# Attention scores of a pair's second head placed earlier in a hand-ordered stream, and the turning of a row placed behind the next row's maximum

## The reference, cut to what matters

```python
proj = h @ w_in
qA, qB = _split_q(proj[..., :Q_W])            # 8 heads dense, 8 heads windowed
z = proj[..., Q_W + KV_W:]
qA = _rope(_rmsnorm(qA, q_norm), cos, sin)
outA = _dense_attention(qA, concat(kA, kA_c), concat(vA, vA_c))     # 512 + 256 keys
outB = _window_attention(_rope(qB, cos, sin), ..., kB_c, vB_c, sink)  # band + 256 keys + sink
y = jnp.concatenate([outA, outB], axis=-1) * jax.nn.silu(z)
x = x + gate * _rmsnorm(y @ w_out, post_g)
```

## Time and profile before

| what | value |
|---|---|
| median of 3 runs (lowest to highest) | 2538.4 us (2538.25 to 2538.62) |
| the profiled execution, its own time | 2538.08 us |
| its span, first to last instruction | 2536.3 us |
| mean granted TensorE clock | 0.985 of full |
| PE busy | 2467.2 us, 97% of the span |
| DVE busy | 1672.1 us, 66% |
| ACT busy | 986.2 us, 39% |
| the attention heads, by the trace | 257.7 to about 810 us |

### The profile page before, as it was taken

One profiled execution on the slowest core, in us unless ns is written; L12 is line 12 of the kernel. 1 busy time (PEld: TensorE's weight loads), 2 busy tenths in 40 slices (PEclk: granted clock), 3 DMA queues, 4 the chain that ended last, 5 costly groups with the idle time before them and its releaser, 6 DMA issues.

```text
span 2536.3 us, 29369 instructions
## 1 busy us (share of the span) xinstructions
PE 2467.2 (97%) x11527; PEld 1991.3 (79%) x11527; DVE 1672.1 (66%) x2570; ACT 986.2 (39%) x1517; POOL 111.6 (4%) x117
## 2 busy tenths in 40 slices
PE   7999899999989999999999999999999999999999
PEld 4789777777766887888888888888888787887887
DVE  4457767778776778776877777456455577656622
ACT  4232544444444333433324333445355433333421
POOL 0000000000000114000000213000000000000000
PEclk8999999999999999999999999999999999999999
DMA  9966677778776764666654754422222245532342
GB/s 349 333 205 208 189 210 204 215 225 222 199 195 177 263 199 150 199 207 208 208 175 155 260 184 142 125 83 84 80 87 83 78 144 172 167 96 83 127 155 83
DMA packets 345660, 439.32 MB, mean 173 GB/s; under 512 B 13154, under 2 KB 271842, under 8 KB 339762
## 3 DMA queue, kind: packets, MB, share of 16 engines
q1 hardware_dynamic: 338048, 403.82, 51.6%
q0 software_dynamic: 5808, 32.84, 3.4%
q10 hardware_dynamic: 1666, 0.79, 0.1%
HBM read 395.44 MB, written 40.37 MB: 172 GB/s over the span
## 4 chain that ended last, share of the span: by engine, by line
PE 79%; DVE 11%; ACT 4%; issue 2%; DMA 2%; SPq 1%; ACTq 0%; POOL 0%; DVEq 0%; POOLq 0%
PE G L2234 68%; PE ST L2234 11%; DVE MACC L1694 2%; DVE SM L1932 2%; DVE WLO L1688 2%; DVE PB L1959 1%; ACT PB L1499 1%; DMA MORE<-in_ev_mod_w 1%; DVE Y L1688 1%; ACT PB L1326 1%; DVE TT L1688 1%; DMA MRAW<-in_ev_mod_w 1%; ACT SQ L1323 1%; DVE QR L1688 0%; PE ST L2237 0%
## 5 line engine op out<-in xcount | busy, mean ns | idle before, releaser
L2234 PE MATMUL G<-HHI,WHI 128*128 128x512 f32 x2596 | 1051.5, 407 | 9.3 <-DVE HLO L1688 7.1
L2234 PE MATMUL G<-HLO,WHI 128*128 128x512 f32 x2560 | 1003.7, 392 | 1.9 <-DVE HLO L1694 1.9
L2234 PE MATMUL G<-HHI,WLO 128*128 128x512 f32 x2560 | 1003.6, 392 | 0.0
L1326 ACT ACTIVATE WHI<-RAW 128x1024 fp32r<-128x1024 f32 x376 | 396.2, 1054 | 604.7 <-PE G L2234 541.5
L2234 PEld LDWEIGHTS G<-HHI,WHI 128*128 128x128 f32 x2596 | 493.3, 190 | 120.9 <-DVE HLO L1688 9.2
L2234 PEld LDWEIGHTS G<-HLO,WHI 128*128 128x128 f32 x2560 | 484.8, 189 | 108.6 <-issue 7.4
L2234 PEld LDWEIGHTS G<-HHI,WLO 128*128 128x128 f32 x2560 | 483.6, 189 | 104.4
L1688 DVE TENSOR_TENSOR WLO<-RAW,WHI 128x1024 fp32r<-128x1024 f32 x376 | 461.7, 1231 | 106.0 <-ACT WHI L1326 105.8
L1694 DVE SCALAR_TENSOR_TENSOR MACC<-MWIDE,SC,MACC 128x512 f32<-128x512 f32 x420 | 317.3, 755 | 88.9 <-DMA MWIDE<-in_w_ada 45.9
L2234 PE MATMUL G<-WHI,HHI 128*128 128x512 f32 (+1 forms) x384 | 143.7, 374 | 0.6 <-ACT K L1326 0.6
L2234 PE MATMUL G<-WLO,HHI 128*128 128x512 f32 (+1 forms) x384 | 136.6, 356 | 0.0
(11 more groups left out here) (273 smaller groups left out, 2461.8 us busy)
## 6 DMA issues: line engine op xcount, KB each, us to landing
RAW<-in_w_in SPq DMA_DIRECT2D x128, 512.0 KB, 3.7
MWIDE<-in_od_mod_w SPq DMA_DIRECT2D x96, 512.0 KB, 4.6
MWIDE<-in_w_ada SPq DMA_DIRECT2D x96, 512.0 KB, 4.7
RAW<-in_ev_w_in SPq DMA_DIRECT2D x80, 512.0 KB, 7.3
RAW<-in_od_w_in SPq DMA_DIRECT2D x64, 512.0 KB, 3.8
p_spill<-PB SPq DMA_DIRECT2D x15, 1536.0 KB, 6.9
PT<-p_spill SPq DMA_DIRECT2D x60, 384.0 KB, 7.1
MWIDE<-in_ev_mod_w SPq DMA_DIRECT2D x32, 512.0 KB, 4.3
```

The lines of the kernel that those rows point to most:

```text
L1326: return e.o.activation(o, i, ACT.Copy, scale=scale)
L2234: return e.o.matmul(o, l, r, start=start, stop=stop, skip_group_check=True)
```

## The change

Only the order of stages changes; no instruction is added or removed.

- The second head's rows stand at steps 20, 23, 26, 29 (three sooner) in pairs 0 to 6, and at 21, 24, 27, 30 (one sooner) in pair 7.
- `row_turn` of rows 0 to 2 stands behind `softmax` of the next row of the same head, so three steps behind its own row in place of two, and behind the next maximum on DVE. The fourth row's stays two steps behind.
- `q_stat` stands at step 4, behind `q_split`, in place of step 3.
- The second head's `turn` comes three steps sooner with its rows and its `turn_in` one step sooner; its `pv` and `gate` come one step sooner (steps 21 and 22 of the next pair). The first head's `turn`, `turn_in`, `pv` and `gate` stay where they were. For head 14 `pv` comes one step sooner, for head 15 it stays.
- `y_split` of heads 4 to 11 in the attention layer follow each other step by step, so head 5 one step sooner, head 6 two, head 7 three and heads 8 to 11 four.

```diff
@@ pair_task
-            if p < 4:
-                put("q_stat", p)
             yield
             if p == 0:
                 put("k_split", 0)
             put("q_split", 2 * p)
+            if p < 4:
+                put("q_stat", p)
             yield
@@
             for n in range(8):
-                later(3 * n + (0 if n < 4 else 5 if p < 7 else 4), "rows", n)
+                later(3 * n + (0 if n < 4 else 2 if p < 7 else 3), "rows", n)
@@
                         put("score", h, qt)
                         put("softmax", h, qt, n)
+                        if qt > 0:
+                            put("row_turn", h, qt - 1)
                         later(t + 1, "row_end", h, qt, n)
-                        later(t + 2, "row_turn", h, qt)
                         if qt == 3:
+                            later(t + 2, "row_turn", h, qt)
                             later(t + 4, "turn", h)
                             if h < 15:
-                                later(t + 8, "turn_in", h)
-                            later(t + (10 if h == 15 else 14 if h == 14 else 23 - i), "pv", h)
+                                later(t + 8 + 2 * i, "turn_in", h)
+                            later(t + (11 if h == 15 else 13 if h == 14 else 23 + i), "pv", h)
@@ first_splits
-                if k < 4 or (k % 2 == 1 if layer == 3 else k < 8):
+                if k < 4 or (k % 2 == 1 if layer == 3 else layer == 2 and k < 8):
                     yield
```

## The result

The changed kernel takes **2551.9 us** (median of 4 runs, 2551.5 to 2552.2) against 2538.3 us for the kernel before in the same session (4 runs, 2536.4 to 2538.6). The ratio is 1.0055, with 1.0038 to 1.0072 at 95%: 13.6 us slower. The forecast was 2564 us with a range of 2538 to 2578. So the direction was right and the size was not: the loss is about half of what was forecast (13.8 us by the spans of the two profiled executions, against 25.5).

The account below looks back on a forecast made before the run. TensorE, busy 97% of the span, was taken as the bound, with time to win only in pauses and lower clock. Changes by pair summed to +25.5 us on 2538.1, so 2563.6, forecast as 2564 us, range 2538 to 2578.

Parts of the forecast that it names:

- What bounds the kernel: TensorE is busy 97% of the span, so time can be won only in its pauses or lower clock, about 61 us.
- Part 3: Pairs 1 to 6: second head's exponential waits for the spill, delaying the gate; PE pauses 4.85 us dense, 7.2 to 8.3 banded.
- What would show it: Signs: PE pauses before odd heads' score row 1 until DVE's gate; exponential starts at spill landing; ACT SQ waits shrink to pair 0's.
- The clock: Lower TensorE clock with each new pause: 3.2 us for 4.85 us, 4.0 us for banded ones; bounds nothing and 4.9.
- Left: What a pair takes when PE never waits, from the earlier windows less pause and clock: 58.3 to 65.0 us.
- The end: Sooner splits remove most of 7.1 us, but head 15's score row 1 waits some 8 us: 1 us slower.
- Pair 0: Ends as before on ACT, with `q_stat` one step later and no gate pause: 1.9 us less.
- Parts 1 and 2: Earlier rows would win most of 45 us of pauses and clock; `row_turn`'s place saves 4 to 6 us DVE idleness a pair.
- (a): Rival: the gate is in time, pauses shrink and the gains show, some 25 us faster, 2513 us; chance 0.12.
- (b): Rival: the gate pauses come but the clock stays up, 21.6 us of clock terms fall away, 2542 us; chance 0.1.
- (c): Rival: DVE is not relieved, next pair's Q stays late too, adding 12 to 17 us, 2578 us; chance 0.1.
- (d): Rival: the same gains and losses nearly cancel, with a shorter spill and half the clock cost, 2545 us; chance 0.08.

Follow-up runs that it names:

- gate_first: Changed kernel with `pv` and gate of the odd heads one step sooner, the gate ahead of `row_end` and `silu_a` on DVE: 2518.9 us.
- gate_with_pv: Changed kernel with only the gate of the odd heads one step sooner, in the step of its `pv`, which stays: 2518.5 us.
- spill_twice: Changed kernel with each spill of PB issued twice, the extra copy first, into DRAM that nothing reads: 2588.2 us.
- turn_splits_stat: Kernel before with the new `row_turn` place, new `y_split` order and `q_stat` at step 4, all but the earlier second head: 2490.5 us.
- turn_only: Kernel before with the new place of `row_turn` alone: 2497.1 us.
- early_only: Changed kernel with `row_turn` and `y_split` put back, leaving the earlier second head and `q_stat`'s move: 2569.4 us.
- splits_only: Kernel before with the new order of `y_split` alone: 2536.0 us.
- turn_one_sooner: turn_only with the second head's rows, `turn` and `turn_in` one step sooner in pairs 0 to 6, its `pv` and gate staying: 2501.9 us.

## Why the prediction was right or wrong, step by step

**What bounds the kernel** was right: PE's busy time didn't move, its pauses and its clock did.

**Part 3, the chain,** was right in each link for heads 3 to 13 and, in pair 1, nearly in its length (13.72 us for 13.6, of which the spill 7.14 for 7.06). The pauses stand before score row 1 of the odd heads with DVE's gate as their releaser, the exponential starts with the landing, and the waits for ACT's squares shrank to the one of pair 0, as "What would show it" asked. gate_first and gate_with_pv showed the link from gate to score (33 us), spill_twice the link from spill to exponential and on to the gate. For head 15 "behind its own spill" was wrong in the main (0.56 of 8.04 us). In pairs 4 to 6 the pause is 1.9 to 3.5 us longer than the exponential's wait for the spill (an estimate of what would stay without that wait).

**The terms.** turn_splits_stat gives what is left of a pair without pause and at full clock, as the busy time of PE in its windows. The pause of the changed kernel is length less busy time, and what then remains is the cost of the clock:

| pair | forecast: left + pause + clock | measured |
|---|---|---|
| 1 | 64.7 + 4.85 + 3.2 | 64.5 + 4.0 + 2.6 = 71.1 |
| 2 | 64.7 + 4.85 + 3.2 | 64.4 + 4.2 + 2.8 = 71.4 |
| 3 | 62.9 + 4.85 + 3.2 | 62.6 + 4.2 + 3.0 = 69.8 |
| 4 | 60.2 + 7.2 + 4.0 | 59.4 + 7.7 + 2.9 = 70.0 |
| 5 | 58.3 + 8.3 + 4.0 | 58.2 + 8.9 + 2.0 = 69.1 |
| 6 | 59.0 + 8.3 + 4.0 | 58.4 + 9.6 + 3.6 = 71.6 |

Over the six pairs the pauses were right in their sum (38.4 us forecast, 38.5 measured; 0.6 to 0.8 too high in each dense pair, 0.5 to 1.3 too low in the others). In pair 6 that is luck: the gate's pause is 6.5 us for 8.3, and 3.0 us for the low part of Q, which the forecast had not, make up for it. **The clock was mis-sized**: 16.9 us for 21.6, or 4.7 too much. The price was taken as (1 - PEclk) x length from the earlier trace rows, and that also counts the part of the low clock that lies inside a pause, where it costs nothing. In pair 1 it gives 3.6 us where 2.6 were lost, and the 4.03 us of its pause at a granted clock of 0.78 account for the 0.9 between them. "Left" was 2.2 us too high for the same six pairs, since it came from windows that had small losses of their own.

**The end** had the wrong sign: -2.8 us for +1.0. The two effects named are both there, score row 1 of head 15 waits 8.04 us ("some 8"), and no wait for high and low parts of the heads is left of the 7.1 us. They cancel: the pauses of the window are 9.4 us before and 9.35 after. What is won is clock, since PE's busy time falls from 66.7 to 63.8 us for the same work, and for that the forecast had no term. This is 3.8 us of the miss. **Pair 0** gave 0.6 us more than taken, with `q_stat`'s pause at 3.5 us from 6.54. That it came so near is luck: the other moved stages take 11.2 us off this pair (turn_splits_stat), and the earlier second head puts 8.6 back, though the forecast saw no loss there. With 6.6 us in the six pairs, 3.8, 0.6, and 0.7 outside the pairs these are the 11.7 us between 25.5 and 13.8.

**Parts 1 and 2 were wrong in what they credited**, and this did not show in the sum. Part 1 gave the pauses between pairs to the second head's place ("rows three sooner ... would cover the waits ... and most of the others"). The runs say otherwise: the turn's place alone takes most of them away (turn_only, -40 us), and earlier rows bring the wait for ACT's squares in pair 0 back, from 0.7 us to 2.5 with one step and 5.1 with two. The step that failed is the sentence that the turn is worth something on PE's path "only if DVE is what PE waits for", read as if the waits put down to ACT were not DVE's. They were. ACT's `q_copy` stands behind the exponential of the second head's last row, that behind DVE's maximum, and that behind the turn of an earlier row, for which DVE stood idle until ACT had scaled it. The "4 to 6 us less DVE idleness a pair" were about right (2.5 to 8.3 us, mostly 3.6 to 6.5), but they pass on to PE, and what they save in clock comes on top. That ACT's and DVE's order hands the idle time on in this way is read from the timelines; that the turn's place gives the 40 us is shown. In the changed kernel they are hidden for the most part, probably since the gate's pause lets DVE and ACT catch up anyway; early_only shows what they still pay there (17.5 us, with the splits).

**The rivals.** (a), the gate in time, fell: the wait for the spill was 3.8 to 5.1 us in pairs 1 to 6. (b), pauses without the clock's cost, fell by the 0.93 to 0.95 in every window, though its 2542 us lies a little nearer to the measured 2551.9 than the forecast does. (c), both sets of pauses, fell in the changed kernel; early_only, with the turn in its old place, has 1.4 us before a next pair's Q, and its other waits for Q are of another kind. (d), 2545 us, is the nearest of the four, and had in part the right reason: the clock cost less than forecast, if not half as much, but the spill was not shorter. The Trainium skill's "DMA: Bandwidth & Descriptors", in its two cost components, would have given the spill an estimated 5.6 us and the whole a time near 2554, close to the measured one. The page fits those figures to transfers that GpSimd issues, and this store is issued by SP. That closeness is an accident: the changed kernel's spills took 7.1 to 7.3 us in the dense pairs and 6.2 to 8.5 in the others, so the trace does not agree, and the smaller loss came from the clock, from "left" and from the end.

## What to carry to other kernels

Before moving work forward in a queue that is served in order, find what it will wait for (here a store from the only tile) and then every stage of other work that now stands behind that wait, on its own engine and on the next; the worst of them here was the one that frees a bank, and it belongs ahead. A dependent operation goes behind independent work that covers its producer, as the turn goes behind the next maximum; a wait put down to one engine is followed back to what that engine stood for. Try each part of a bundle alone: here a gain of 48 us lay under a loss of 61.

## What the runs showed of the hardware

- **A pause of TensorE does not cost a fixed time in clock.** In the changed kernel one pause of 4.0 to 4.2 us went with a PEclk of 0.95 in its window, and pause and clock together cost 6.7, 6.9 and 7.2 us. But 4.9 and 5.0 us in pairs 1 and 3 of early_only went with 0.98; the pause of 3.0 us in pair 2 with 0.98 in the kernel before and 0.95 in splits_only; one of 2.5 us in pair 0 of turn_one_sooner with 0.95, and ones of 2.3 and 2.4 us in pairs 5 and 6 of turn_splits_stat with 1.00. Four pauses of 0.7 to 2.7 us in pair 5 of gate_first, 7.0 us together, left it at 1.00. What decides between these was not looked for.
- **A store's time moves with its place.** The same 1536 KB took 7.1 us in pair 1, but 8.5, 8.5 and 8.0 us for heads 8, 10 and 12 of the changed kernel, where head 10 took 7.63 before, and 8.7 for head 8 in gate_with_pv. What it met there was not looked for. A second store of the same size, issued 0.38 us ahead of it, made it land 3.5 to 3.8 us later (pairs 1 to 3 of spill_twice).
- **The loss has a knee.** One step sooner (about 1.4 us) costs 5 us and two cost 44. It fits that the slack of the spill in turn_only was 3.6 us in pairs 1 to 3 and at most 1.4 in the banded ones, and that only with two steps the gate stands behind the exponential. By the spans (39 us between these two profiled executions), pair 0 has 8 of them, pairs 1 to 3 10 and pairs 4 to 6 24, against 28 us of pauses for the gate; no run took the parts apart.
